# Late keys in one run, scores right behind the first turn, exponentials ahead of the copies, in the first attention's later heads

## The reference

```python
s_s = jnp.einsum("bqgrd,bgqksd->bgrqks", qb, kg) - slopes[..., None] * dist_s
p_s = masked_softmax(s_s, mask_s)
o_s = jnp.einsum("bgrqs,bgqsd->bqgrd", p_s, vg)
s_w = jnp.einsum("bqgrd,bkgd->bgrqk", qb, kwb) - slopes * dist_w
p_w = masked_softmax(s_w, mask_w)
o_w = jnp.einsum("bgrqk,bkgd->bqgrd", p_w, vwb)
out = gb[..., 0:1] * o_c + gb[..., 1:2] * o_s + gb[..., 2:3] * o_w
...
x = x + mix @ w_out
```

## Time and profile before

| | |
|---|---|
| median of 3 runs | 754.82 us (753.05 to 755.27) |
| the profiled execution's own time | 755.52 us |
| its span, first to last instruction | 753.7 us |
| PE busy | 733.9 us (97%) |
| DVE busy | 539.1 us (72%) |
| ACT busy | 377.4 us (50%) |
| mean granted clock of PE | 0.993 |
| stretch of the later heads | 105 to 144 us of the span |

### The profile page before, as it was taken

One profiled execution on the slowest core, in us unless ns is written; L12 is line 12 of the kernel. 1 busy time (PEld: TensorE's weight loads), 2 busy tenths in 40 slices (PEclk: granted clock), 3 DMA queues, 4 the chain that ended last, 5 costly groups with the idle time before them and its releaser, 6 DMA issues.

```text
span 753.7 us, 13081 instructions
## 1 busy us (share of the span) xinstructions
PE 733.9 (97%) x5264; PEld 676.4 (90%) x5264; DVE 539.1 (72%) x926; ACT 377.4 (50%) x542; POOL 51.2 (7%) x72
## 2 busy tenths in 40 slices
PE   5999999999999999999999999999999999999996
PEld 4999986789999999998999999999988998998995
DVE  6798787586677777756758988785967876555554
ACT  7433767756334333445545346664634544444442
POOL 1950000000000000000333000000000000000000
PEclk9999989999999999999999999999999999999999
DMA  8636411288778878843355456555632675644611
GB/s 334 226 120 230 162 57 57 73 335 327 287 295 319 313 300 306 306 142 112 114 179 177 168 173 235 205 202 195 238 154 87 249 257 190 215 161 180 223 57 56
DMA packets 27021, 151.08 MB, mean 200 GB/s; under 512 B 3128, under 2 KB 7836, under 8 KB 9564
## 3 DMA queue, kind: packets, MB, share of 16 engines
q1 hardware_dynamic: 22620, 124.81, 46.0%
q10 hardware_dynamic: 3456, 25.17, 8.3%
q0 software_dynamic: 896, 0.43, 0.3%
HBM read 148.92 MB, written 1.05 MB: 199 GB/s over the span
## 4 chain that ended last, share of the span: by engine, by line
PE 90%; DVE 6%; issue 1%; ACT 1%; DMA 1%; SPq 0%; DVEq 0%; ACTq 0%
PE ps L467 27%; PE ps L468 26%; PE ps L469 26%; PE ps L574 2%; PE ps L773 2%; PE ps L598 1%; DMA raw<-wts 1%; DVE w_lo L1644 1%; PE ps L1023 1%; DVE rows_ga L1783 1%; PE ps L1009 0%; PE ps L608 0%; PE ps L686 0%; PE ps L999 0%; PE ps L969 0%
## 5 line engine op out<-in xcount | busy, mean ns | idle before, releaser
L1644 DVE TENSOR_TENSOR w_lo<-raw,w_hi 128x2048 fp32r<-128x2048 f32 x106 | 239.9, 2268 | 109.3 <-ACT w_hi L1202 109.2
L467 PE MATMUL ps<-h_hi,w_hi 128*128 128x256 f32 (+2 forms) x1000 | 284.9, 285 | 0.6 <-DVE h_lo L1696 0.6
L468 PE MATMUL ps<-h_lo,w_hi 128*128 128x256 f32 (+2 forms) x1000 | 282.8, 283 | 0.0
L469 PE MATMUL ps<-h_hi,w_lo 128*128 128x256 f32 (+2 forms) x1000 | 282.8, 283 | 0.0
L1202 ACT CAST w_hi<-raw 128x2048 fp32r<-128x2048 f32 x106 | 198.8, 1887 | 47.3 <-PE ps L469 46.5
L467 PEld LDWEIGHTS ps<-h_hi,w_hi 128*128 128x128 f32 (+2 forms) x1000 | 190.2, 190 | 3.3 <-issue 2.1
L468 PEld LDWEIGHTS ps<-h_lo,w_hi 128*128 128x128 f32 (+2 forms) x1000 | 190.2, 190 | 1.2
L469 PEld LDWEIGHTS ps<-h_hi,w_lo 128*128 128x128 f32 (+2 forms) x1000 | 190.2, 190 | 0.3
L467 PE MATMUL ps<-w_hi,mix_hi 128*128 128x512 f32 x248 | 97.4, 393 | 1.2 <-DVE small L1783 0.8
L468 PE MATMUL ps<-w_lo,mix_hi 128*128 128x512 f32 x248 | 96.8, 390 | 0.0
L469 PE MATMUL ps<-w_hi,mix_lo 128*128 128x512 f32 x248 | 96.5, 389 | 0.0
(11 more groups left out here) (307 smaller groups left out, 899.0 us busy)
## 6 DMA issues: line engine op xcount, KB each, us to landing
raw<-wts SPq DMA_DIRECT2D x109, 1024.0 KB, 4.8
ada<-w_ada ACTq DMA_DIRECT2D x24, 1024.0 KB, 5.4
alibi<-wts SPq DMA_DIRECT2D x2, 1024.0 KB, 7.0
fa_whole<-wts SPq DMA_DIRECT2D x2, 1024.0 KB, 6.1
resid<-x SPq DMA_DIRECT2D x2, 512.0 KB, 4.2
raw<-wts SPq DMA_DIRECT2D x2, 512.0 KB, 6.7
rows_ga<-rows_wide SPq DMA_DIRECT2D x1, 1024.0 KB, 6.9
out<-resid SPq DMA_DIRECT2D x4, 256.0 KB, 2.0
```

Of the source, the lines that this page charges most:

```text
L467: nc.tensor.matmul(o, lh, rh, start=start, stop=False)
L468: nc.tensor.matmul(o, lh, rl, start=False, stop=False)
L469: return nc.tensor.matmul(o, ll, rh, start=False, stop=stop)
L1644: V.tensor_tensor(w_lo[:, s % RING, 0:w], raw[:, n_of[name] % RAW, 0:w], w_hi[:, s % RING, 0:w].bitcast(F32), ALU.subtract).then_inc(w_rea ...
```

## The change

On PE, `late_keys(1)` moves up directly behind `late_keys(0)`. In the loop over pairs, `scores` moves from ahead of turn(2j) to behind it, and one pair further: in turn j it was pair j+1, and is now pair j+2, ahead of `values(j-1)`. On ACT, exp(4) and exp(5) come together behind the copies of head 1, and from then on the copies of head n are followed by exp(n+4) (before, from n = 4, by exp(n+2)), and `keep_mix` comes behind that exponential where it was ahead of it. On DVE, the three copies of the compressed probabilities (`pcT`) come behind `masked(4)` and `normal(3)`. No instruction is added or taken away.

```diff
--- before.py
+++ after.py
@@ -704,6 +704,7 @@
             i.then_inc(pcT_ps, 1)
             pe.wait_ge(z_evac, s_idx["vw"] + 1)
             late_keys(0)
+            late_keys(1).then_inc(pe_tile, 1)
 
             def out0_part(kk):
 
@@ -717,17 +718,15 @@
                 return i
 
             for j in range(1, NQ // 2):
-                if 2 <= j < NQ // 2 - 1:
-                    pe.wait_ge(s_sb, 8 * (j + 1))
-                    if j == 2:
-                        pe.wait_ge(z_evac, s_idx["k1"] + 1)
-                    scores(j + 1)
                 if j == 1:
                     pe.wait_ge(pcT_ready, 3)
                 probs_turn(2 * j)
+                if j < NQ // 2 - 2:
+                    pe.wait_ge(s_sb, 8 * (j + 2))
+                    if j == 1:
+                        pe.wait_ge(z_evac, s_idx["k1"] + 1)
+                    scores(j + 2)
                 values(j - 1)
-                if j == 1:
-                    late_keys(1).then_inc(pe_tile, 1)
                 probs_turn(2 * j + 1)
                 if j >= NQ // 2 - 2:
                     if j == NQ // 2 - 2:
@@ -1329,15 +1328,14 @@
                 for br in range(2):
                     act.wait_ge(pT_ps, 2 * n + br + 1)
                     nc.scalar.copy(turned_of[n % 4][:, 384 * br:384 * (br + 1)], ps[:, 4 + br, 0:384]).then_inc(pTn_ready, 1)
+                if n == 1:
+                    attn(4)
+                    attn(5)
+                    copy_out(s_idx["k1"])
+                if 2 <= n < NQ - 4:
+                    attn(n + 4)
                 if n % 2 == 0 and n >= 2:
                     keep_mix(n // 2 - 1)
-                if n == 1:
-                    attn(4)
-                if n == 2:
-                    attn(5)
-                    copy_out(s_idx["k1"])
-                if 4 <= n < NQ - 2:
-                    attn(n + 2)
             after(s_idx["vw"])
             keep_mix(NQ // 2 - 1)
             after(s_idx["k1"])
@@ -1848,13 +1846,14 @@
             V.tensor_tensor(pcmp[:, :, :, 0:CMP_SLOT], scmp, wide(mx), ALU.mult).then_inc(pc_ready, 1)
             after(8)
 
-            dve.wait_ge(pcT_ps, 1)
-            for c in range(3):
-                V.tensor_copy(pcT[:, c, :], ps[:, 4 + c // 2, (c % 2) * T:(c % 2 + 1) * T]).then_inc(pcT_ready, 1)
             for n in range(4, NQ):
                 dve.wait_ge(pT_ps, 2 * (n - 3))
                 masked(n)
                 normal(n - 1)
+                if n == 4:
+                    dve.wait_ge(pcT_ps, 1)
+                    for c in range(3):
+                        V.tensor_copy(pcT[:, c, :], ps[:, 4 + c // 2, (c % 2) * T:(c % 2 + 1) * T]).then_inc(pcT_ready, 1)
                 if n == 5:
                     for c in range(2):
                         dve.wait_ge(chi_ready, c + 1)
```

## The result

The changed kernel took 756.59 us (median of 6 runs, 756.48 to 756.89), the kernel before 754.07 us in runs beside it: ratio 1.0036, 95% interval 1.0025 to 1.0047. Twelve further runs of the changed kernel gave 755.75 us against 754.06, ratio 1.0023 (1.0013 to 1.0034). The forecast was 757.2 us and 2.36 us more than before; the two comparisons give 2.5 and 1.7 us more.

A forecast was written before the change was run, and what follows sets the result against it. PE, busy 97% of the span, was taken as the bound. In the later heads 23.94 us of work and 6.01 of waits put out0_part(0) 2.36 us later; on the median of 754.82 that gives 757.2 us, range 754.7 to 759.6.

The forecast's parts named there:

- The bound: PE, busy 97% of the span: only 3.65 us of waits can change, and gain or loss is passed on whole.
- the stretch: PE's work in the later heads, from first late key to out0_part(0): 27.59 us before, 29.95 forecast.
- three waits of 2.17 us: PE's waits for DVE's maxima before scores(4), scores(5) and out0_part(0): 0.67, 0.70, 0.80 us; forecast to go, longer ones replacing them.
- Late keys in a row: PE from 105.32: same 48 matmuls with nothing to wait for, ending at 111.25; scores(3) at 112.18, 2.63 us earlier.
- The margin: ACT before scores(3): masked(5) taken 2 us earlier, exp(5) ends at 110.0, over 1 us to spare.
- Exponentials ahead of the copies: ACT's copies of head 3 stand behind exp(6) and keep_mix(0), so turn(4) waits 1.42 us; likewise turn(6) and turn(8).
- The chain over nsa_lo: DVE's nsa_lo(0), ahead of masked(7), waits for keep_mix(0): scores(4) waits 0.37 us, period 6.67 us against 6.15.
- the lead is kept: Rival, 14%: keep_mix and nsa_lo hide beside other work, period stays 6.15 us, out0_part(0) 1.3 later, 756.1 us.
- the period: Time from start of scores(4) to start of scores(5) on PE: 6.67 us forecast against 6.15 before.
- The end of the heads: Behind scores(5): values(2), turn(7) added, head 8's copies behind exp(11); out0_part(0) at 135.27, 2.36 us later.
- The clock: Rival, 10%: PE's granted clock falls to half again around its waits, costing 1.5 to 3.0 us, 758.7 to 760.2 us.
- The absolute time: Whole kernel: 2.36 us carried on unchanged to the end, 757.2 us against the median of 754.82.

The follow-up runs named there:

- control: The kernel before once more, unchanged, timed against the kernel before: 754.12 us against 754.09, ratio 1.0001.
- copies_only: Changed kernel with, on ACT alone, the copies of the odd head ahead of the exponential: 762.06 us, ratio to the kernel before 1.0094.
- scores5_back: Changed kernel with scores(5) back behind turn(7) on PE: 760.05 us (4 runs), ratio to the kernel before 1.0077.
- keep_first: Changed kernel with keep_mix ahead of the exponential on ACT, as before the change: 757.34 us, ratio to the kernel before 1.0038.

## Why the prediction was right

Counted from the start of the first late key, the steps were forecast and came so (us):

| | forecast | measured |
|---|---|---|
| scores(3) | 6.86 | 6.76 |
| turn(4) | 12.42 | 12.35 |
| scores(4) | 13.53 | 13.45 |
| scores(5) | 20.20 | 20.14 |
| turn(9) | 29.21 | 29.18 |
| out0_part(0) | 29.95 | 29.83 |
| out1 | 41.11 | 40.99 |

*The bound.* That the stretch is passed on whole holds: 11.16 us behind it in both kernels, and 620.8 and 620.9 us from `out0_part(0)` to the end. Of the three waits of 2.17 us two shrank to 0.20 each and the third went.

*Late keys in a row.* Right in the place of `scores(3)`; done alone, this part is worth 0.22 us of the stretch. The margin was wrong: I gave exp(5) over 1 us to spare, and there was none. ACT moved the late keys out right behind exp(5), and just in time for `scores(3)` at 110.78:

```profile
110.06 0.58 ACT L1267 COPY z<-ps 128x512 f32<-128x512 f32 x1
```

The forecast found its margin in a wait of DVE in the profile of before:

```profile
105.60 1.09 DVE L1853 COPY misc<-ps 128x256 f32<-128x256 f32 x3 [3.06 <-PE ps L702]
```

Exp(5) ended about 6.0 us behind the start of the first late key, where 4.7 was forecast. The profile that the steps were read from had the fall of the clock at 91 us, so that PE was late in it and DVE idle. In the control's profile, without the fall, the same wait is 0.66 us; and `masked(5)` came 0.7 us earlier against the first late key than before (2.98 us behind it for 3.72), not the 2 us that were taken. So the margin came from one slow stretch of one run, and it was luck that exp(5) still ended just in time.

*Exponentials ahead of the copies.* Right in place and size: 1.45 us from the end of turn(3)'s slot to turn(4) (114.18 + 0.74 to 116.37) for 1.42. No single edit of its surroundings helps: with the PE order alone, the ACT order alone, or `keep_mix` alone put otherwise, the stretch grew. PE's and ACT's order together took these waits away.

*The chain over nsa_lo.* Right, 6.69 us for 6.67. The forecast's rival "the lead is kept" asked that `keep_mix` and `nsa_lo` hide beside other work, and they don't: DVE waits 0.85 us for `keep_mix` in each round. `nsa_lo` one head later brings the period to 6.43 us and the time to 754.16.

*The end of the heads.* Right: 9.69 us from `scores(5)` to `out0_part(0)` for a forecast of 9.75, against 6.21 before. The forecast gave this two grounds, two more steps on PE, and the copies of head 8 behind exp(11). The second is the one that can be mended: with the copies of head 8 ahead of exp(11) and the two steps kept it is 7.52 us, with no wait left. Taking the two steps away alone is no cure, since `scores(5)` then comes 3 us later.

*The clock.* In the changed kernel it stayed at 1.00 from 99 us to the end of the stretch, with waits of 1.3 us. Its price and its being near were real, though: where a wait of 2.96 or 4.01 us came up, the clock fell behind it. The Trainium skill, page "TensorE: Matmul & The Clock Gate", section "HAM oscillation — how this bites in real kernels", says that gaps in which PE idles long enough bring the clock down, and that the work behind them starts at the lower one. These two runs agree with the first half. As to the second, the clock fell within 0.2 us of the first work behind the 4.01 us (0.85 in the slice from 131 to 132), but only 1.4 us into the work behind the 2.96 us (scores from 119.22; 0.80 in the slice from 120 to 121). The rule that the prediction cites from the section "A second HAM failure mode: psum-queue depth-cycling" of the same page of the Trainium skill, short idles between groups of matmuls, did not come true here: waits of 1.3 and 0.2 us in every 6.69 left the clock at 1.00.

*The absolute time.* 757.2 forecast, 756.59 and 755.75 measured. The 0.6 to 1.4 us are not in the stretch (0.12 us off). They come mostly from the median of three runs that I started from, 754.82, of a kernel whose runs lie in groups at 753.0 and 754.7 with a few above 755; how near 757.2 a median of six runs comes is a matter of luck, of which groups they fall into.

## What to carry to other kernels

Lay a changed order out by the starts in the trace, engine by engine, and look for the cycle: here it ran through three queues, and the wait that was largest in the profile (copies, 1.3 us) was not the link that set the period (`nsa_lo` ahead of `masked`). Of five single edits four made the stretch longer and one (`nsa_lo`) made it 1.3 us shorter, and only the edits on all three queues together beat the kernel before; so when a reorder fails, look in the other engines' queues for what still stands in its old place. Lay out the end of a software pipeline by itself: here 2.17 us were to be had behind `scores(5)` with the period left as it was. Read the steps from a second profile too, since one with a slow stretch shows idle time in the other engines that isn't there in the next run. Put a result that nothing soon waits for (here the low part of the output) behind, not ahead of, the instruction that the next step waits for.

## What the runs showed of the hardware

The granted clock of PE fell to half (1.2 GHz) behind waits of 2.96 us (twice, copies_only) and 4.01 us (scores5_back) within busy code, and not behind waits of 1.3 us (changed kernel) and 1.9 us (keep_first) that came every 7 us. One such fall cost 1.5 us there (`values` at 3.43 instead of 1.89). Behind the 48 matmuls of 16 columns the clock fell in some runs and not in others, at 2.6 us in the profile of before. In code that is the same from run to run, the matmuls at 14 us were spaced by 0.12 us in some profiles and 0.21 in others, and the first late key came about 1.6 us later in the latter; a comparison of a few runs can be off by as much.
